# A two-layer encoder on one core: token block 0 ahead of block 1 at each norm, attentions begun inside their projections, modulation rows and spare products taken off TensorE

## The chip, the cores and the metric

The kernel runs on one core of a Trainium2 chip. The core has TensorE (PE, matmuls), VectorE (DVE), ScalarE (ACT), GpSimd (POOL) and SyncE (SP, which here issues the weight transfers), each with its own instruction stream; they wait for each other on semaphores. The metric is the device time of one execution in microseconds (us), the median of several runs.

## The reference, cut to what matters

256 tokens of width 1024 go through two layers. Every sub-layer is modulated by rows computed from a conditioning vector c.

```python
x = x + gate * diff_attention(modulate(rms_norm(x, g), shift, scale), ...)   # layer 0, mixer A, 8 heads, 2 maps each
x = x + gate * swiglu(modulate(...), w_in, w_out)                            # layer 0, dense, D_FF = 2816
k, v = split(modulate(rms_norm(x, g), shift, scale) @ w_kv)                  # one shared K/V set
x = x + gate * window_attention(modulate(...), w_q, sinks, w_o, k, v)        # layer 1, mixer B, 16 heads
x = x + gate * moe_swiglu(modulate(...))                                     # layer 1, top 2 of 8 experts
```

Each shift, scale and gate is a row `c @ ada_w[:, 1024 columns] + ada_b`. In mixer B a head's softmax is `exp(l - m) / (sum(exp(l - m)) + exp(sink - m))` with `m = max(max(l), sink)`. Attention is causal by chunks of 64 tokens, so queries of tokens 0 to 127 see no key behind token 127.

## The kernel before, in words

**Tiling.** The tokens are two blocks of 128 (`TB` = 2; X, H and Q are 128 x 2 x 1024). Weights come as fp32 tiles of 128 x 1024 in a ring of 12 slots (WRAW). ACT rounds each to fp32r (`hi`, tile WHI, L642), DVE takes the rest (`lo`, tile WLO, L970), and PE multiplies every tile three times (WHI by the high and low parts of the activations, WLO by the high part; all recorded at L1471). The activations are transposed on PE (L1501), split into HT_HI by ACT (L704) and into HT_LO by DVE (L1036, L1038, four operations of 512 columns).

**Stages, in the order in which every engine's stream is written:** start and first norm; QKV (24 tiles); attention A (16 steps, block 0's eight heads first); WO (8 tiles); the residual and the norm; FFN (11 steps of 4 input and 2 output tiles); residual and norm; KV (4 tiles); a second norm; BQ (8); attention B (16 steps); BO (8); norm; router; MoE (56 steps of 8 + 4 tiles). WO, BQ and BO are `project`: for each weight tile both token blocks, 12 products of 128 x 512, so that both blocks end with the last tile. Behind each projection DVE runs `residual` (L1119, L1120, two of each), `rms` with ACT's squares (L655) and root (L671), `norm` (L1025, L1027, two of each); PE transposes H when both blocks are there, and its next product waits for all four HT_LO.

**Modulation rows.** A row is the sum of 8 pieces (128 x 1024 of ada_w times c). Most pieces are one operation each on DVE: `early_product` (L984) up to WO, and `products` (L995) in FFN, where POOL brings them into SHR; `FF_PRODUCTS` says how many go into each FFN step. A row so made is summed over partitions by PE (`mod_sums`, MOD times ones) and copied by ACT (`mod_rows`, L698). Three rows are made on PE itself, as WRAW times c in two halves a piece: row scale_f of layer 0 in attention A and gate_f of layer 1 in attention B (`row_pieces`, nine products a half, one or two per attention step), and scale_f of layer 1 behind FFN (`ada_on_pe`, 18 products).

**Spare products.** `keep_clock` issues products that nobody reads, 24, 40, 24 and 44 of them: ahead of WO, behind WO, behind BQ and behind BO.

```python
            mod_sums(3, MOD0[3], 2)
            keep_clock(0, 40)
            pe.wait_ge(mod_ready, MOD_READY_EARLY)
            ht_transposes(H, h_ready, (5, 6))
            pe.wait_ge(ht_lo, 12)
```

**Attention step n.** PE makes head n + 3's logits, the transposes of n's probabilities and the values' product of n - 1; DVE adds the bias to head n + 2's logits (L1068), takes the negated maximum (L1074 in A, L1077 and a minimum with the sinks, L1078, in B), then n's totals (L1088 to L1091 in A; L1094, L1095 in B), and in B scales the output of n - 2 (L1100); ACT takes the exponentials (L726; in B two of the sinks at L723 as well) and copies.

## Time and profile before

| what | value |
|---|---|
| median of 3 runs | 1586.43 us (1586.08 to 1592.24) |
| the profiled execution's own time | 1585.24 us |
| its span, first to last instruction | 1583.4 us |
| mean granted TensorE clock | 0.978 of full |
| TensorE busy | 1500.0 us |
| VectorE busy | 1282.0 us |
| ScalarE busy | 983.4 us |

The profiled execution took 1.84 us more than its span, and 1.19 us less than the median. Busy time doesn't count waits, so an engine's share says how full its stream is, not that it sets the end.

### The profile page before, as it was taken

What the parts mean: (1) busy time and instruction counts of PE and PEld (TensorE: products, weight loads), DVE (VectorE), ACT (ScalarE), POOL (GpSimd) and SP (SyncE); (2) the same over time, 40 slices, a digit from 0 to 9 for tenths busy, and PEclk for the clock granted to TensorE, in tenths of its full rate; (3) what the DMA queues carried; (4) which work ended last, traced back from release to release, by engine and by line L of the source; (5) the groups of instructions that cost most, each with busy time, mean ns of one, the idle gap of its engine ahead of it and who ended that gap; (6) DMA issues with size and microseconds to landing.
All of it is one profiled execution on the core that took longest, in us unless ns stands there. A gap on an engine that the chain in (4) does not pass through costs nothing.

```text
span 1583.4 us, 22553 instructions
## 1 busy us (share of the span) xinstructions
PE 1500.0 (95%) x6706; PEld 1192.2 (75%) x6706; DVE 1282.0 (81%) x1396; ACT 983.4 (62%) x1276; POOL 83.6 (5%) x119
## 2 busy tenths in 40 slices
PE   5898989999978996999999999999999999999997
PEld 2784768777656575888888888888888888888886
DVE  5776758788655655989989989989989989989997
ACT  2466423444335623678778778778778778778774
POOL 3000121111010000000000000000000000000100
PEclk9999989999989998999999999999999999999999
DMA  9972479898474332999999999999999999999994
GB/s 344 347 275 73 145 251 371 296 348 310 152 231 145 113 125 83 343 373 369 395 379 370 394 380 365 396 377 367 398 378 370 392 376 372 381 376 370 398 392 167
DMA packets 212226, 494.33 MB, mean 312 GB/s; under 512 B 16434, under 2 KB 39186, under 8 KB 212178
## 3 DMA queue, kind: packets, MB, share of 16 engines
q1 hardware_dynamic: 198000, 444.66, 77.0%
q0 software_dynamic: 13376, 47.03, 8.5%
q10 hardware_dynamic: 802, 2.06, 0.3%
q8 instruction: 25, 0.41, 0.1%
q14 instruction: 23, 0.18, 0.0%
HBM read 487.13 MB, written 6.55 MB: 312 GB/s over the span
## 4 chain that ended last, share of the span: by engine, by line
PE 88%; DVE 7%; DMA 2%; ACT 2%; issue 1%; SPq 0%; DVEq 0%; ACTq 0%
PE PS L1471 85%; DMA WRAW<-in_ada_w 2%; PE PS L1861 2%; DVE HT_LO L1036 1%; DVE WLO L970 1%; PE PS L1569 1%; DVE MOD L995 0%; ACT WHI L642 0%; DVE ss L1045 0%; PE PS L1839 0%; DVE H L1025 0%; DVE X L1120 0%; DVE H L1027 0%; DVE Q L1054 0%; PE PS L1700 0%
## 5 line engine op out<-in xcount | busy, mean ns | idle before, releaser
L970 DVE TENSOR_TENSOR WLO<-WRAW,WHI 128x1024 fp32r<-128x1024 f32 x790 | 915.5, 1218 | 92.6 <-ACT WHI L642 92.4
L642 ACT ACTIVATE WHI<-WRAW 128x1024 fp32r<-128x1024 f32 x790 | 778.4, 1052 | 100.1 <-PE PS L1471 64.0
L1471 PE MATMUL PS<-WHI,HT_HI 128*128 128x512 f32 x1280 | 513.6, 401 | 26.8 <-DVE WLO L970 12.7
L1471 PE MATMUL PS<-WLO,HT_HI 128*128 128x512 f32 x1280 | 504.4, 394 | 0.0
L1471 PE MATMUL PS<-WHI,HT_LO 128*128 128x512 f32 x1280 | 431.1, 394 | 0.0
L1471 PEld LDWEIGHTS PS<-WHI,HT_HI 128*128 128x128 f32 x1280 | 244.0, 191 | 79.2 <-DVE HT_LO L1036 12.2
L1471 PEld LDWEIGHTS PS<-WHI,HT_LO 128*128 128x128 f32 x1280 | 243.5, 190 | 52.9
L1471 PEld LDWEIGHTS PS<-WLO,HT_HI 128*128 128x128 f32 x1280 | 244.3, 191 | 48.5
L1471 PE MATMUL PS<-WHI,AT_HI 128*128 128x512 f32 x536 | 214.2, 400 | 4.4 <-DVE WLO L970 3.0
L1471 PE MATMUL PS<-WHI,AT_LO 128*128 128x512 f32 x536 | 209.5, 391 | 0.0
L1471 PE MATMUL PS<-WLO,AT_HI 128*128 128x512 f32 x536 | 209.5, 391 | 0.0
L921 ACT ACTIVATE AT_HI<-PS 128x512 fp32r<-128x512 f32 x56 | 33.5, 599 | 190.1 <-PE PS L1861 190.1
L1471 PEld LDWEIGHTS PS<-WHI,AT_HI 128*128 128x128 f32 x536 | 101.1, 189 | 28.5 <-issue 4.6
L1471 PEld LDWEIGHTS PS<-WLO,AT_HI 128*128 128x128 f32 x536 | 101.0, 188 | 23.7 <-issue 2.9
L1471 PEld LDWEIGHTS PS<-WHI,AT_LO 128*128 128x128 f32 x536 | 101.0, 188 | 21.1
L1395 DVE TENSOR_TENSOR AT_LO<-PS,AT_HI 128x512 fp32r<-128x512 f32 x56 | 38.7, 692 | 72.2 <-ACT AT_HI L921 72.2
L995 DVE SCALAR_TENSOR_TENSOR MOD<-SHR,condT,MOD 128x1024 f32<-128x1024 f32 x56 | 71.6, 1278 | 0.6
L1471 PE MATMUL PS<-WRAW,condT 128*128 128x512 f32 x108 | 56.5, 640 | 2.1 <-DMA WRAW<-in_ada_w 2.1
L836 ACT ACTIVATE AT_HI<-PS 128x512 fp32r<-128x512 f32 x11 | 6.6, 599 | 63.7 <-PE PS L1700 63.7
L610 POOL DMA_DIRECT2D y_rows<-MOD x7 | 4.0, 574 | 797.1 <-DVE MOD L1382 797.1
L1471 PE MATMUL PS<-MOD,CST 128*128 128x512 f32 x64 | 35.5, 666 | 9.0 <-DMA MOD<-in_ada_b 5.4
L1391 DVE TENSOR_TENSOR MOD<-MOD,PS 128x512 f32<-128x512 f32 x56 | 38.0, 679 | 6.4 <-ACT MOD L917 6.4
(209 smaller groups left out, 880.5 us busy)
## 6 DMA issues: line engine op xcount, KB each, us to landing
WRAW<-in_moe_w_in SPq DMA_DIRECT2D x448, 512.0 KB, 6.3
WRAW<-in_moe_w_out SPq DMA_DIRECT2D x224, 512.0 KB, 5.5
WRAW<-in_ada_w SPq DMA_DIRECT2D x56, 512.0 KB, 6.9
WRAW<-in_ffn_w_in SPq DMA_DIRECT2D x88, 256.0 KB, 5.8
SHR<-in_ada_w POOLq DMA_DIRECT2D x40, 512.0 KB, 6.4
WRAW<-in_a_w_qkv SPq DMA_DIRECT2D x24, 512.0 KB, 16.3
WRAW<-in_ffn_w_out SPq DMA_DIRECT2D x22, 512.0 KB, 5.9
SHR<-in_kv_ada_w POOLq DMA_DIRECT2D x16, 512.0 KB, 6.1
```

The lines of the kernel that those rows point to most:

```text
L610: pool.dma_start(Y_ROWS.ap()[e * P:(e + 1) * P, :], Y).then_inc(y_stored, 16)
L642: nc.scalar.activation(WHI[:, u.split(k), :], WRAW[:, u.raw(k), :], ACT.Copy).then_inc(w_hi, 1)
L836: nc.scalar.activation(AT_HI[:, :], PS[:, 2, :], ACT.Copy).then_inc(at_hi, 1)
L921: nc.scalar.activation(AT_HI[:, :], PS[:, 2, :], ACT.Copy).then_inc(e_at_hi, 1)
L970: V_.tensor_tensor(WLO[:, u.split(k), :], WRAW[:, u.raw(k), :], f32(WHI[:, u.split(k), :]), ALU.subtract).then_inc(w_lo, 1)
L995: V_.scalar_tensor_tensor(row, ADA[:, k % ADA_SLOTS, :], condT[:, k:k + 1], row, ALU.mult, ALU.add).then_inc(ada_used, 1)
L1036: V_.tensor_tensor(dst, PS[:, b, :], high, ALU.subtract).then_inc(ht_lo, 1)
L1391: V_.tensor_tensor(EACT, ESIL, PS[:, 1, :], ALU.mult).then_inc(e_act, 1)
L1395: V_.tensor_tensor(AT_LO[:, :], PS[:, 2, :], f32(AT_HI[:, :]), ALU.subtract).then_inc(e_at, 1)
L1471: return nc.tensor.matmul(out, a, b, start=start, stop=stop)
L1569: last = nc.tensor.transpose(PS[:, 4 + n % 2, at:at + P], s_buf(a, n)[:, m, kt * P:(kt + 1) * P], ident)
L1861: last = nc.tensor.transpose(PS[:, 2, c * P:(c + 1) * P], EACT[:, c * P:(c + 1) * P], ident)
```

## The change

1. The four `keep_clock` calls go (132 products).
2. Row scale_f of layer 1 goes to DVE's `products` in FFN (`FF_PRODUCTS` of the last four entries 7 for 5), and POOL loads its pieces. Of row scale_f of layer 0, pieces 0 to 3 go to DVE in QKV (`SCALE_AT`), 4 to 7 stay on PE (`scale_pieces`). Row gate_f goes to DVE behind attention B (`gate_products`).
3. WO, BQ and BO are `project_by_block`: tiles 0 and 1 for both blocks, tiles 2 to 7 for block 0, then the same for block 1. FFN's last two tiles are ordered so too. `residual`, `rms` and `norm` run per block, the norm in halves of 512 columns, each of which releases four transposes; a projection's first products wait for their own HT_LO alone.
4. Attention A's first four heads' logits are issued among V's last tiles. Inside BQ's block 1, block 0's queries are transposed and heads 0 and 1 get their logits; block 1's queries are transposed in attention step 1. In both attentions block 0's outputs are normed or transposed ahead of the last steps.
5. In B the sink is a 129th (257th) logits column: a zero in PSUM and the sink in the bias tile. The exponential's sum then holds it; four small operations a head go.
6. POOL issues the small loads of the start after ten DVE products, and the attention's bias load after six `lo`.

```diff
-FF_PRODUCTS = (6, 6, 6, 6, 6, 6, 5, 5, 5, 5)
+FF_PRODUCTS = (6, 6, 6, 6, 6, 6, 7, 7, 7, 7)
...
+SCALE_PE = tuple((SCALE_F0, k) for k in range(4, KT))
 GATE_AT = tuple(range(4, 20, 2))
+SCALE_AT = (17, 19, 21, 23)
...
-    order += list(range(U_FF, U_KV)) + [("scale_f", k) for k in range(KT)]
-    order += list(range(U_KV, U_BO + 5)) + [("gate_f", k) for k in range(KT)]
+    order += list(range(U_FF, U_BO + 5)) + [("gate_f", k) for k in range(KT)]
...
                     for m in range(2):
-                        if a == "B":
-                            nc.scalar.activation(c[:, 6 + m:7 + m],
-                                                 sinks[:, 2 * (n % HEADS) + m:2 * (n % HEADS) + m + 1], ACT.Exp,
-                                                 bias=c[:, 2 + m:3 + m], scale=-1.0)
-                        nc.scalar.activation(buf[:, m, 0:span], buf[:, m, 0:span], ACT.Exp,
+                        nc.scalar.activation(buf[:, m, 0:cols], buf[:, m, 0:cols], ACT.Exp,
                                              bias=c[:, 2 + m:3 + m],
                                              accum_out=c[:, 4 + m:5 + m]).then_inc(sems["expd"], 1)
 
...
+                    if n == 1 and a == "B":
+                        transposed(10, lambda n: Q[:, 1, n * 512:n * 512 + 512], 3, (6, 7), qkt_psum)
...
+            def gate_products(*ks):
+
+                row = MOD[:, LATE_SLOTS[LATE_GATE_F], :]
+                for k in ks:
+                    place = PLACE["gate_f", k]
+                    dve.wait_ge(w_landed[place % RAW_SLOTS], landed_at(place))
+                    dve.wait_ge(ada_used, DVE_FF + k)
+                    V_.scalar_tensor_tensor(row, WRAW[:, place % RAW_SLOTS, :], condT[:, k:k + 1], row,
+                                            ALU.mult, ALU.add).then_inc(ada_used, 1)
...
-            def norm(scale_slot, shift, gains):
+            def norm(i, scale_slot, shift, gains):
 
                 dve.wait_ge(gain_used, gains)
-                for i in range(TB):
-                    chain(V_.scalar_tensor_tensor(H[:, i, :], X[:, i, :], nx[:, i, 1:2], MOD[:, scale_slot, :],
-                                                  ALU.mult, ALU.mult))
-                    V_.tensor_tensor(H[:, i, :], H[:, i, :], shift, ALU.add
+                for half in range(2):
+                    cols = slice(half * 512, half * 512 + 512)
+                    chain(V_.scalar_tensor_tensor(H[:, i, cols], X[:, i, cols], nx[:, i, 1:2],
+                                                  MOD[:, scale_slot, cols], ALU.mult, ALU.mult))
+                    V_.tensor_tensor(H[:, i, cols], H[:, i, cols], shift[:, cols], ALU.add
                                      ).then_inc(h_ready, 1)
...
+            dve.wait_ge(block_out, 1)
+            dve.wait_ge(mod_ready, MOD_READY_EARLY - 2)
+            residual(0, MOD0[2])
+            fold(MOD0[4], MOD[:, MOD0[4], :], 2)
+            rms(0, 3)
+            dve.wait_ge(mod_ready, MOD_READY_EARLY)
...
-            dve.wait_ge(mod_ready, MOD_READY_EARLY - 2)
-            residual(lambda i: pair(4 + 2 * i), MOD0[2], lambda i: H[:, i, :])
-            fold(MOD0[4], MOD[:, MOD0[4], :], 2)
-            rms(4)
-            dve.wait_ge(mod_ready, MOD_READY_EARLY)
-            norm(MOD0[4], MOD[:, MOD0[3], :], 2)
+            residual(1, MOD0[2])
+            lo(u, 32)
+            rms(1, 4)
...
             lo(u, *range(0, 6))
+            dve.wait_ge(mod_ready, MOD_READY_EARLY + 2 * LATE_SHIFT_F)
+            fold(MODKV[1], MOD[:, MODKV[1], :], 3)
+            dve.wait_ge(block_out, 2)
+            residual(0, MOD0[5])
             dve.wait_ge(w_used, U_KV)
-            dve.wait_ge(mod_ready, MOD_READY_EARLY + 2 * LATE_SHIFT_F)
-            residual(lambda i: pair(4 + 2 * i), MOD0[5], lambda i: H[:, i, :])
...
-            norm(MOD1[1], MOD[:, MOD1[0], :], 4)
-            head_norm(7, 4, 64, lambda i: heads_of(PS[:, 4 + i, 0:256], 4),
-                      lambda i: [KDUP[:, i, :, c, :] for c in range(2)], kdup_ready)
+            for i in range(TB):
+                norm(i, MOD1[1], MOD[:, MOD1[0], :], 4)
+            u = Units(U_BQ)
+            lo(u, 0, 1)
             ht_los(4)
-            u = Units(U_BQ)
-            lo(u, *range(0, 13))
-            head_norm(9, 16, 64, lambda i: heads_of(pair(4 + 2 * i), 16),
...
+            biased("B", 0)
+            biased("B", 1)
+            head_norm(1, 9, 16, 64, W4[:, :], [(heads_of(Q[:, 1, :], 16), heads_of(pair(6), 16), 0, 16)], qk_norm)
             attention("B")
             ht_los(5)
-            lo(u, *range(13, 20))
+            lo(u, 12, 13)
+            gate_products(0, 1, 2)
+            lo(u, 14)
+            gate_products(3, 4)
+            lo(u, 15)
+            gate_products(5, 6, 7)
             dve.wait_ge(wr_hi_ready, 1)
...
+            def project_by_block(u, bank, splits, between):
+
+                project(u, 0, bank, range(0, 2), splits)
+                if (0, 1) in between:
+                    between[0, 1]()
                 for i in range(TB):
-                    pe.wait_ge(ready, counts[i])
-                    for k in range(KT):
+                    for k in range(2, KT):
+                        if i == 0:
+                            split_ready(u, k)
+                            pe.wait_ge(ht_lo, splits + k // 2 + 1)
+                        last = block_products(u, k, i, bank)
+                        if i:
+                            last.then_inc(w_used, 1)
+                            if (1, k) in between:
+                                between[1, k]()
+                    if i == 0:
+                        last.then_inc(block_out, 1)
...
-            def keep_clock(bank, count):
-
-                for _ in range(count):
-                    mm(PS[:, bank, :], HT_HI[:, 0, 0:P], HT_HI[:, 0:2, :].rearrange("p k s -> p (k s)"))
...
+            def scale_pieces(n):
+
+                for half, steps in enumerate(SCALE_STEPS):
+                    cols = slice(half * 512, half * 512 + 512)
+                    for at, k in steps:
...
-            attention("A")
-            mod_sums(2, MOD0[2], 4)
+            logits("A", 0, 1)
+            project(u, 2 * KT, 4, range(6, 7))
+            logits("A", 2)
+            project(u, 2 * KT, 4, range(7, 8))
+            logits("A", 3)
+            attention("A", 4)
+            mod_sums(DVE_QKV, MOD0[2], 4)
+            ht_transposes(Q, h_parts(1, BLOCKS[:2]))
             pe.wait_ge(attn["A"]["o_ready"], TB * HEADS)
-            keep_clock(0, 24)
-            ht_transposes(Q, h_ready, (3, 4))
-            pe.wait_ge(ht_lo, 8)
+            ht_transposes(Q, h_parts(1, BLOCKS[2:]))
             pe.wait_ge(mod_ready, MOD_READY_EARLY - 2)
-            project(Units(U_WO), 0, 4)
-            mod_sums(3, MOD0[3], 2)
-            keep_clock(0, 40)
+            project_by_block(Units(U_WO), 4, 4, {(1, 3): lambda: mod_sums(DVE_EARLY, MOD0[3], 2)})
             pe.wait_ge(mod_ready, MOD_READY_EARLY)
-            ht_transposes(H, h_ready, (5, 6))
-            pe.wait_ge(ht_lo, 12)
-
-            def f_in(u, k0, ks, first, last):
+            ht_transposes(H, h_parts(2, BLOCKS[:2]))
+            ht_transposes(H, h_parts(2, BLOCKS[2:]))
...
-            mod_sums(ADA_EARLY + LATE_SHIFT_F, MOD1[3], 2)
-            ada_on_pe(0, 0)
+            mod_sums(DVE_FF - KT, LATE_SLOTS[LATE_SHIFT_F], 0)
+            mod_sums(DVE_FF, LATE_SLOTS[LATE_SCALE_F], 2)
             pe.wait_ge(mod_ready, MOD_READY_EARLY + 2 * (LATE_SCALE_F + 1))
-
-
-            ht_transposes(H, h_ready, (7, 8))
-            pe.wait_ge(ht_lo, 16)
+            ht_transposes(H, h_parts(3, BLOCKS[:2]))
+            pe.wait_ge(x_new, 4)
+            ht_transposes(H, h_parts(3, BLOCKS[2:]))
...
-            keep_clock(3, 24)
...
-            keep_clock(3, 44)
...
+            def first_queries():
+
+                pe.wait_ge(qk_norm, 5)
+                block_transposes(Q, 0, 4, qkt_psum)
+
+            def first_logits():
+
+                pe.wait_ge(qkt_ready, 10)
+                pe.wait_ge(kbt_ready, 2)
+                pe.wait_ge(sink_cols, 1)
+                logits("B", 0, 1)
+
+            project_by_block(Units(U_BQ), 4, 16,
+                             {(0, 1): kbt_transposes, (1, 5): first_queries, (1, 6): first_logits})
+            logits("B", 2)
+            attention("B", 3)
+            ht_transposes(Q, [(1, half, attn["B"]["o_ready"], HEADS + 4 * half + 4) for half in range(2)])
+            project_by_block(Units(U_BO), 4, 20, {})
+            ht_transposes(H, h_parts(5, BLOCKS[:2]))
+            pe.wait_ge(x_new, 6)
+            mod_sums(DVE_FF + KT, LATE_SLOTS[LATE_GATE_F], 6)
+            ht_transposes(H, h_parts(5, BLOCKS[2:]))
```

**VectorE around WO's end.** H<-PS and X<-X,H are the residual, nx the root's scalars, H<-X,nx,MOD and H<-H,MOD the norm. Of before:

```order
L970 TENSOR_TENSOR WLO<-WRAW,WHI 128x1024 [waits w_hi] x4
L1119 TENSOR_TENSOR H<-PS,MOD 128x1024 [waits mod_ready,w_used]
L1120 TENSOR_TENSOR X<-X,H 128x1024 [waits dve_chain]
L1119 TENSOR_TENSOR H<-PS,MOD 128x1024
L1120 TENSOR_TENSOR X<-X,H 128x1024 [waits dve_chain]
L1018 SCALAR_TENSOR_TENSOR MOD<-MOD,S 128x1024 [waits gain_landed]
L1007 TENSOR_SCALAR nx<-nx 128x2 [waits x_squares]
L1010 RECIPROCAL nx<-nx 128x2 [waits root_ready]
L1025 SCALAR_TENSOR_TENSOR H<-X,nx,MOD 128x1024 [waits gain_used,mod_ready,dve_chain]
L1027 TENSOR_TENSOR H<-H,MOD 128x1024 [waits dve_chain]
L1025 SCALAR_TENSOR_TENSOR H<-X,nx,MOD 128x1024
L1027 TENSOR_TENSOR H<-H,MOD 128x1024 [waits dve_chain]
L1036 TENSOR_TENSOR HT_LO<-PS,HT_HI 128x512 [waits ht_hi] x4
```

Of the change, from the residual of block 1 on (block 0's residual, scalars and norm stand in the nine rows ahead):

```order
L1144 TENSOR_TENSOR H<-PS,MOD 128x1024 [waits w_used]
L1145 TENSOR_TENSOR X<-X,H 128x1024 [waits dve_chain]
L997 TENSOR_TENSOR WLO<-WRAW,WHI 128x1024 [waits w_hi]
L1044 TENSOR_SCALAR nx<-nx 128x1 [waits x_squares]
L1047 RECIPROCAL nx<-nx 128x1 [waits root_ready]
L1063 SCALAR_TENSOR_TENSOR H<-X,nx,MOD 128x512 [waits gain_used,dve_chain]
L1065 TENSOR_TENSOR H<-H,MOD 128x512 [waits dve_chain]
L1063 SCALAR_TENSOR_TENSOR H<-X,nx,MOD 128x512
L1065 TENSOR_TENSOR H<-H,MOD 128x512 [waits dve_chain]
L997 TENSOR_TENSOR WLO<-WRAW,WHI 128x1024 [waits w_hi]
L1074 TENSOR_TENSOR HT_LO<-PS,HT_HI 128x512 [waits ht_hi] x4
```

Half of the residual and of the norm has moved ahead of the wait for WO's last tile; three of four `lo` now follow it.

**TensorE behind FFN's last product.** MOD,CST are sums of rows over partitions, WRAW,condT pieces of a row, CST,H transposes. Of before (the first five of the eight pairs of pieces):

```order
L1471 MATMUL PS<-WHI,AT_LO 128x512
L1471 MATMUL PS<-MOD,CST 128x512 [waits ada_used,mod_ready]
L1471 MATMUL PS<-MOD,CST 128x512
L1471 MATMUL PS<-MOD,CST 128x512 [waits modb_landed]
L1471 MATMUL PS<-MOD,CST 128x512
L1471 MATMUL PS<-WRAW,condT 128x512 [waits w_landed6]
L1471 MATMUL PS<-WRAW,condT 128x512
L1471 MATMUL PS<-WRAW,condT 128x512 [waits w_landed7]
L1471 MATMUL PS<-WRAW,condT 128x512
L1471 MATMUL PS<-WRAW,condT 128x512 [waits w_landed8]
```

Of the change:

```order
L1540 MATMUL PS<-WHI,AT_LO 128x512
L1540 MATMUL PS<-MOD,CST 128x512 [waits ada_used,mod_ready]
L1540 MATMUL PS<-MOD,CST 128x512
L1540 MATMUL PS<-MOD,CST 128x512 [waits ada_used]
L1540 MATMUL PS<-MOD,CST 128x512
L1597 MATMUL PS<-CST,H 128x128 [waits h_ready,mod_ready]
L1597 MATMUL PS<-CST,H 128x128 x3
L1597 MATMUL PS<-CST,H 128x128 [waits h_ready]
L1597 MATMUL PS<-CST,H 128x128 x3
```

The two sums of row scale_f took the place of 18 products, and the transposes go in four parts.

**VectorE between attention B and the residual behind BO.** Of before:

```order
L1100 TENSOR_TENSOR Q<-PS,sm 128x128 [waits pv_B] x2
L1036 TENSOR_TENSOR HT_LO<-PS,HT_HI 128x512 [waits ht_hi] x4
L970 TENSOR_TENSOR WLO<-WRAW,WHI 128x1024 [waits w_hi] x7
L1271 TENSOR_TENSOR wr_lo<-wr,wr_hi 128x64 [waits wr_hi_ready]
L1119 TENSOR_TENSOR H<-PS,MOD 128x1024 [waits w_used]
L1120 TENSOR_TENSOR X<-X,H 128x1024 [waits dve_chain]
L1119 TENSOR_TENSOR H<-PS,MOD 128x1024
```

Of the change:

```order
L1128 TENSOR_TENSOR Q<-PS,sm 128x128 [waits pv_B] x2
L1074 TENSOR_TENSOR HT_LO<-PS,HT_HI 128x512 [waits ht_hi] x4
L997 TENSOR_TENSOR WLO<-WRAW,WHI 128x1024 [waits w_hi] x2
L1021 SCALAR_TENSOR_TENSOR MOD<-WRAW,condT,MOD 128x1024 [waits ada_used,w_landed11]
L1021 SCALAR_TENSOR_TENSOR MOD<-WRAW,condT,MOD 128x1024 [waits ada_used,w_landed0]
L1021 SCALAR_TENSOR_TENSOR MOD<-WRAW,condT,MOD 128x1024 [waits ada_used,w_landed1]
L997 TENSOR_TENSOR WLO<-WRAW,WHI 128x1024 [waits w_hi]
L1021 SCALAR_TENSOR_TENSOR MOD<-WRAW,condT,MOD 128x1024 [waits ada_used,w_landed2]
L1021 SCALAR_TENSOR_TENSOR MOD<-WRAW,condT,MOD 128x1024 [waits ada_used,w_landed3]
L997 TENSOR_TENSOR WLO<-WRAW,WHI 128x1024 [waits w_hi]
L1021 SCALAR_TENSOR_TENSOR MOD<-WRAW,condT,MOD 128x1024 [waits ada_used,w_landed4]
L1021 SCALAR_TENSOR_TENSOR MOD<-WRAW,condT,MOD 128x1024 [waits ada_used,w_landed5]
```

Eight products of gate_f stand among the `lo` of BO's tiles 4 to 7.

## Rows read from the trace of the kernel before

**Rows 1.** The page's fourth part: the chain that ended last, share by engine.

```profile
PE 88%; DVE 7%; DMA 2%; ACT 2%; issue 1%; SPq 0%; DVEq 0%; ACTq 0%
```

**Rows 2.** Windows cut at TensorE's starts: length, busy by engine, PEclk, DMA share, GB/s.

```profile
46.53:121.38 74.85, 72.70 (x338) 59.99 (x339) 55.14 (x67) 39.28 (x56) 0.95 (x1) 0.98 0.86 308
125.33:172.38 47.05, 40.90 (x191) 23.45 (x190) 32.16 (x79) 31.66 (x94) 4.55 (x4) 0.96 0.32 101
172.38:212.76 40.38, 36.53 (x156) 29.05 (x157) 32.94 (x31) 13.86 (x18) 3.82 (x4) 0.96 0.64 206
212.76:418.51 205.75, 196.56 (x836) 155.75 (x837) 152.28 (x140) 79.25 (x99) 30.42 (x58) 0.98 0.84 299
418.51:448.66 30.15, 26.43 (x81) 14.86 (x81) 19.43 (x21) 11.54 (x17) 3.14 (x5) 0.94 0.66 178
461.53:493.81 32.28, 26.95 (x121) 22.52 (x120) 20.72 (x27) 18.04 (x26) 0.00 (x0) 0.89 0.58 204
493.81:554.67 60.86, 53.05 (x301) 34.40 (x299) 36.60 (x109) 40.45 (x131) 0.57 (x1) 0.97 0.28 85
554.67:595.07 40.40, 35.84 (x157) 29.09 (x157) 22.33 (x24) 12.18 (x18) 1.09 (x2) 0.96 0.38 121
641.44:1583.40 941.96, 934.03 (x4239) 771.27 (x4237) 847.09 (x792) 706.28 (x776) 17.90 (x16) 1.00 1.00 371
```

**Rows 3.** The chain of work, WO's products to FFN's first: start, length, what.

```profile
172.38 23.69 PE PS L1471 x96
...
196.09 1.24 DVE H L1119
...
204.06 1.30 DVE H L1025
...
210.22 2.49 DVE HT_LO L1036 x4
```

**Rows 4.** PE's timeline before FFN; in brackets the idle time before, and its releaser.

```profile
197.20 9.68 PE L1471 MATMUL PS<-HT_HI 128*128 128x512 f32 x40
...
212.76 0.50 PE L1471 MATMUL PS<-WHI,HT_HI 128*128 128x512 f32 x1 [2.55 <-DVE HT_LO L1036]
```

**Rows 5.** Windows of 2 us for PE: length, busy, PEclk (granted clock), DMA share, GB/s.

```profile
212.00:214.00 2.00, 1.24 (x5) 1.00 0.34 116
214.00:216.00 2.00, 2.00 (x6) 0.51 0.67 214
```

**Rows 6.** DVE's timeline in attention A, block 1: `biased` of two heads in a row.

```profile
141.92 0.68 DVE L1068 TENSOR_TENSOR S<-PS,SHR 128x512 f32<-128x512 f32 x1
...
147.02 0.69 DVE L1068 TENSOR_TENSOR S<-PS,SHR 128x512 f32<-128x512 f32 x1 [2.85 <-PE PS L1471]
```

**Rows 7.** DVE's timeline in a step of the dense channel mixer.

```profile
300.02 2.67 DVE L995 SCALAR_TENSOR_TENSOR MOD<-SHR,condT,MOD 128x1024 f32<-128x1024 f32 x2
```

**Rows 8.** DVE's timeline at that mixer's end: the split of the last tiles.

```profile
417.14 4.63 DVE L970 TENSOR_TENSOR WLO<-WRAW,WHI 128x1024 fp32r<-128x1024 f32 x4 [0.25 <-ACT WHI L642]
```

**Rows 9.** PE's timeline behind that mixer's last product.

```profile
429.07 13.90 PE L1471 MATMUL PS<-WRAW,condT 128*128 128x512 f32 x32
```

**Rows 10.** The chain from BQ's last product to attention B's first transpose.

```profile
493.81 1.04 ACT W L796
...
507.47 0.64 PE PS L1569 x2
```

**Rows 11.** PE's timeline in attention B, block 1.

```profile
532.16 1.02 PE L1471 MATMUL PS<-WRAW,condT 128*128 128x512 f32 x2
...
533.11 0.70 PE L1471 MATMUL PS<-MOD,Q 64*128 64x256 f32 x4
...
536.08 0.70 PE L1471 MATMUL PS<-MOD,Q 64*128 64x256 f32 x4
```

**Rows 12.** DVE's timeline in attention B, block 1: `biased` of two heads in a row.

```profile
527.99 0.68 DVE L1068 TENSOR_TENSOR MOD<-PS,SHR 128x512 f32<-128x512 f32 x1
...
530.10 0.68 DVE L1068 TENSOR_TENSOR S<-PS,SHR 128x512 f32<-128x512 f32 x1
```

More of the change, by code:

```diff
@@ L1480, in split_ready, with block_products @@
                 pe.wait_ge(w_lo, u.count(k) + 1)
-            def project(u, k0, bank, ks=range(KT)):
+            def block_products(u, k, i, bank):
+                s, rows = u.split(k), slice(i * P, i * P + P)
+                kt = k % KT
+                for half in range(2):
+                    cols = slice(half * 512, half * 512 + 512)
+                    last = split_mm(PS[:, bank + 2 * i + half, :], HT_HI[:, kt, rows], HT_LO[:, kt, rows],
+                                    WHI[:, s, cols], WLO[:, s, cols], kt == 0, kt == KT - 1)
+                return last
@@ L1685, in f_in @@
+            def f_in(u, k0, ks, first, last, splits=None):
                 for k in ks:
```

542 lines of the change are left out of this document (297 added, 245 removed).

## The prediction

> **What bounds the kernel now.** I read the page's chain first: TensorE holds 88% of what ended last, VectorE 7% [rows 1]. Then the stages, cut where TensorE starts [rows 2]. MoE, 942 of 1583 us, keeps PE busy for 934 at full clock with the DMA engines at 1.00; the change alters nothing in it, so it stays. What can move lies ahead of 595 us, and there the stages differ. In FFN PE is busy for 197 of 206 us and DVE for 152: PE is the bound, DVE's slack is small. Between the projections the engines take turns: from WO's first product to FFN's takes 40.38 us, of which WO's products are 23.69, and behind them stand the residual, the norm and four HT_LO [rows 3]. Attention B takes 60.86 us with PE busy for 53, attention A 47.05.
>
> A product costs 0.2275 us at full clock: MoE's window holds 4032 of them and 224 transposes of a quarter of the columns, for which I take half that time each. WO's 96 would be 21.8 us and took 23.69, so a start at half clock costs 1.9 us. The spare products do not prevent it: 40 ran from 197.20 for 9.68 us, the transposes followed, PE paused 2.55 us for HT_LO [rows 4], the granted clock was still 1.00 in the window at 212 and fell to 0.51 in the next, after products had begun again [rows 5]. The Trainium skill ("TensorE: Matmul & The Clock Gate", section "Why this matters for your kernels") advises to keep TensorE fed without pauses between bursts, which speaks against removing the spare products; by these rows they bought nothing at the one place that they were for.
>
> **The change part by part.** All against the profiled execution's 1585.24 us (span 1583.4 and 1.84 around it; 1.2 below the median of the runs).
>
> (a) *Start and QKV: 0.* QKV waits for its first HT_LO instead of four and for half norms: PE may start 4 to 5 us earlier. But DVE takes four more products of 1.28 us (half of 2.67 [rows 7]), 5 us, in a window in which it is busy 55 of 75 us, and the norms of Q and K, for which V's tiles and the logits wait, stand behind them. The later bias load relieves the weights. I let gain and loss cancel; the ends are -5 (all of the start kept) and +3.
>
> (b) *Attention A to WO: -9.* The window is 47.05 [rows 2]. The row's last eight half products remain of sixteen, and are spread: 8 x 0.87 (a half product is two records, 13.90/16 [rows 9]) = 7 us less on PE. Where PE was idle it fell to half clock: DVE waited 2.85 us for one head's logits and the step took 5.10 instead of some 2.2 [rows 6]; I count that once as saved, 2.9, and 2.5 for steps that PE paced. Behind the last step, squares and scalars of block 0 are now done early, the norm releases four transposes at a time and WO waits for one HT_LO (three of four saved, 2.49 for four [rows 3], 1.9): 3.6 in all. Ends -4 (DVE and ACT, busy 32 each, pace all steps) and -11.
>
> (c) *WO to FFN: -6.2.* Block 0's residual (2.46) and norm (2.5) go under block 1's 36 products (8.2 us). PE's 96 products and the sum take 23.7 + 1.7; then come residual of block 1 2.46 [rows 3], a `lo` 1.2, scalars 0.7, norm 2.6, a `lo` 1.2, HT_HI and one HT_LO 0.6 each: 9.4 less 0.6 of overlap with the sum. Together 34.2 against 40.38. The two `lo` that now stand in the chain are price of the new order. Ends -3 (block 0's norm late, behind the sum) and -8. The 40 spare products cost nothing before, since PE waited for the norm anyway; so their going gives nothing here.
>
> (d) *FFN: +6.* Eight more products at 1.28 on DVE: 10.2 us if DVE paced every step. In steps with a sum and 6 products DVE has hardly a pause from tile to tile, two products in a row among them [rows 7]; over the whole stage it is idle for 53 of 206 us [rows 2]. The last four steps get two each. Two of them have a sum and I count +1.9 each; one has none, +0.5; in the last the sum is near and I take +1.7. Ends +4 and +10.2. DMA brings 4 MB more in these steps, on top of 299 GB/s.
>
> (e) *Behind FFN to KV: -10.5.* The window of 30.15 loses 16 half products, 13.90 us [rows 9], and two more that add the bias row, 1.7; two more sums (1.7) come. DVE becomes the chain: `lo` of the six tiles at 1.16 each from 417.14 on [rows 8] end 5.6 us into the window, then fold 1.2, two residuals 4.9, scalars 0.5, two norms 5.1, HT_HI, HT_LO and the last transposes 1.7, some 0.5 between: 19.6. So of the 15.5 taken off PE only 10.5 is seen. Ends -12 (PE paces) and -8.
>
> (f) *KV to BQ's end: 0.* KV's copy frees PSUM and BQ starts some 6 us sooner, but PE then waits for KDUP, whose norm now stands behind two more `lo`, restarts at half clock, and takes on the transposes of block 0's queries and two logits. Ends -3 and +3.
>
> (g) *Attention B: -21*, the largest term. Before, 13.66 us pass between BQ's last product and the first transpose of probabilities [rows 10]: two head norms, the query transposes, `biased`, exponentials. Of that block 0's half now runs in BQ; the window's start to step 2 I count as 10.8, since block 1's head norm, the Exp table and its transposes still come. Block 1's steps were paced by PE at 2.97 us (533.11 to 536.08), of which 0.87 is a piece; without it PE needs 2.1 [rows 11]. DVE's step was 2.11 (527.99 to 530.10) with the two sink operations [rows 12]; without them I take 2.0. Block 0's steps I take at 1.5. So 10.8 + 4 x 1.5 + 8 x 2.0 + the last two 2.6, last product to BO 2.6, half-clock restart 1.9: 39.9 against 60.86. In what is left, 18 half products (15.6 us) are the main thing. Ends -16 and -25.
>
> (h) *BO to router: -5.5.* As (c), but eight gate products of 1.28 stand on DVE between `lo` of BO's tiles. DVE is busy 22.3 of 40.4, so it has the room, yet block 0's residual comes late: its 60 products end at 15.5 (13.6 and a cold start), but DVE has three HT_LO 1.9, four `lo` 4.7, eight products 10.2 and the fold 1.2 ahead of it, 18.3 with the small split of the router's weights. Residual, scalars, squares, norm and a `lo` bring it to 26.3, behind PE's last product at 23.7; the tail as in (c), 8.6, ends at 34.9 against 40.40. 44 spare products cost nothing, PE waited. Ends -2 (the products push the tiles' `lo`, and BO waits) and -8.
>
> (i) Router and MoE: 0. The zero column in PSUM and the copy of the sinks are two small DVE operations in BQ, where DVE is busy for 20.7 of 32.3 us; without that cover they would cost under 1 us.
>
> Sum: 0 - 9 - 6.2 + 6 - 10.5 + 0 - 21 - 5.5 = -46.2, which gives **1539.0 us**. All cheap ends at once would give 1517, all dear ones 1568; since they hardly go together I take 1524 to 1560 for the likeliest case.
>
> **The rivals.**
>
> *Hand-offs move to VectorE and give most back* (0.10). DVE gets 20 products more (25.6 us) and the `lo` stand in the chains of (c), (e), (h). If FFN takes the full +10.2, attention A's steps stay at DVE's pace (-4), (c) and (h) give -3 and -2, (e) -8, (g) -16 and (a) +2: -20.8, 1564 us. For it: DVE is busy 152 of 206 in FFN. Against: it has pauses where the chains lie.
>
> *Slower: TensorE stays at half clock* (0.03). Without spare products the pauses at four hand-offs might leave whole projections slow. A product at half clock costs 0.2 us more; WO, BQ and BO wholly so cost 3 x (96 x 0.2 - 1.9) = 52, so 1591 us. It decides from about 230 products at half clock that are not so now. For it: pauses of 2.5 us precede every fall. Against: the falls happened with the spare products too, and each is over within some 4 us of products, 1.9 us of loss a time [rows 3, 5]. The skill's advice (same page and section) is this rival; the trace does not bear it out.
>
> *More than forecast* (0.05): block 0's chains are wholly hidden and V does not wait for K's norm: all cheap ends but FFN's, -5 - 11 - 8 + 6 - 12 - 3 - 25 - 8 = -66, 1519 us, with 1524 as the near edge. For it: DVE's share between projections is a half. Against: each `lo` in a tail is a wait that was not there.
>
> *The change does little* (0.02): only if the sixteen half products and the pieces had been in shadow already; rows 9 and 11 speak against it, since PE has no gap there.
>
> **How the numbers follow.** The likeliest case has 0.80, at 1539, own range 1524 to 1560. The dear case lies just above, the cheap one just below, so 1524 to 1560 leaves out some 2 in 10 and is my range. A measurement of this kernel tells a change from none at about 0.5%, 8 us. Every case but the second and the last is faster by more: 0.95, and I leave 0.02 for the same and 0.03 for slower.
>
> **What would show each step.** Time from WO's first product to FFN's of 34, from FFN's end to KV's start of 20, from BQ's last product to BO's first of 40; AT transposes in FFN's last four steps 1 to 2 us further apart. In attention B, block 1's logits every 2.0 us. Granted clock back at full within 4 us of every start. The forecast is wrong if DVE's idle time vanishes in QKV or if BQ's block 1 waits for KDUP longer than some 4 us, if gate products hold `lo` of BO's tiles, or if clock rows show 0.5 for a whole projection.

## The result and the profile after

The changed kernel took 1569.17 us (median of 4 runs, 1564.66 to 1575.25) beside 1586.26 for the kernel before: 0.9905 of its time, 95% interval 0.9878 to 0.9931. In a later session of 12 runs it took 1577.84 (1558.46 to 1583.17), 0.9936 [0.9904, 0.9967]. A ratio, here and below, is estimated from the fast runs beside those of the kernel before in the same session and is not the quotient of two medians; one of the 12, 1583.17, counts as slow. The change is faster by 1% or less, 17 us in the first session and some 10 by the ratio of the second, where 46 were forecast, and both times are outside the range of 1524 to 1560. In the later session its single runs scatter over 25 us, those of the kernel before over 12.

The profiled execution took 1564.66 us, span 1562.8. In the chain of work on its profile page VectorE's share has grown from 7% [rows 1] to 12%.

```profile
PE 81%; DVE 12%; issue 2%; DMA 2%; ACT 2%; SPq 0%; DVEq 0%; ACTq 0%
```

The windows, with columns as in [rows 2]. In order: QKV's first product to WO; WO to FFN; FFN; its last tiles to KV; KV to the end of BQ's products; attention B, up to BO's first product; BO to the router; router to MoE's steady part; MoE.

```profile
41.53:162.65 121.12, 107.04 (x496) 77.40 (x497) 94.49 (x155) 71.67 (x154) 5.68 (x7) 0.97 0.68 235
162.65:197.56 34.91, 27.88 (x117) 20.91 (x117) 32.32 (x37) 15.01 (x22) 5.33 (x4) 0.91 0.63 195
197.56:411.14 213.58, 199.50 (x836) 155.07 (x837) 165.40 (x152) 79.74 (x99) 35.54 (x68) 0.98 0.88 315
411.14:431.28 20.14, 15.02 (x48) 10.86 (x49) 18.28 (x24) 10.70 (x18) 3.16 (x5) 0.78 0.94 266
431.28:472.49 41.21, 38.55 (x184) 30.68 (x185) 31.03 (x46) 20.02 (x30) 3.67 (x3) 1.00 0.46 139
472.49:509.73 37.24, 30.89 (x226) 24.24 (x225) 26.24 (x69) 28.86 (x92) 0.57 (x1) 0.95 0.12 42
509.73:545.07 35.34, 29.41 (x117) 21.07 (x118) 32.59 (x38) 13.02 (x21) 1.09 (x2) 0.90 0.70 229
545.07:597.08 52.01, 38.74 (x181) 32.81 (x182) 29.55 (x77) 17.02 (x21) 1.98 (x2) 0.77 0.38 128
597.08:1562.80 965.72, 958.02 (x4243) 771.56 (x4241) 847.23 (x792) 707.23 (x776) 17.79 (x16) 1.00 0.98 362
```

Of the kernel before, the windows that [rows 2] does not have in this cut: KV to the end of BQ's products, attention B, router to MoE's steady part.

```profile
448.66:493.61 44.95, 39.62 (x169) 32.76 (x170) 26.73 (x32) 18.04 (x25) 3.65 (x3) 0.89 0.71 243
493.61:554.67 61.06, 53.25 (x302) 34.59 (x300) 36.60 (x109) 40.45 (x131) 0.57 (x1) 0.97 0.28 85
595.07:641.44 46.37, 35.09 (x185) 29.49 (x186) 26.80 (x73) 14.82 (x18) 1.98 (x2) 0.82 0.34 114
```

| stage | before | after | moved | forecast |
|---|---|---|---|---|
| start to WO (a, b) | 172.38 | 162.65 | -9.7 | -9 |
| WO to FFN (c) | 40.38 | 34.91 | -5.5 | -6.2 |
| FFN (d) | 205.75 | 213.58 | +7.8 | +6 |
| FFN's last tiles to KV (e) | 30.15 | 20.14 | -10.0 | -10.5 |
| KV to BQ's last product (f) | 44.95 | 41.21 | -3.7 | 0 |
| attention B (g) | 61.06 | 37.24 | -23.8 | -21 |
| BO to router (h) | 40.40 | 35.34 | -5.1 | -5.5 |
| router to MoE's steady part | 46.37 | 52.01 | +5.6 | 0 |
| MoE | 941.96 | 965.72 | +23.8 | 0 |

At the router the kernel is 50 us ahead. Then MoE, which the change does not touch, takes 23.8 us more, with the same work (x4243 records beside x4239) at a granted clock of 1.00, as before. In the stretch below TensorE is busy throughout in both kernels and simply makes fewer products. It is the same stretch of MoE in the kernel before and in the changed one, for PE alone (busy, records, clock, DMA share, GB/s). Before:

```profile
700.00:1000.00 300.00, 300.00 (x1371) 1.00 1.02 379
```

After:

```profile
700.00:1000.00 300.00, 300.00 (x1338) 1.00 1.01 374
```

2.4% fewer products in 300 us. The 4032 products of MoE take 23.8/4032 = 0.0059 us more each. The rate is already lower in QKV: from 60 to 110 us the products of HT start 0.233 us apart (mean of those that follow each other without a break), before 0.227.

### The profile page after: what moved, and what is told of

It is laid out like the page before. It is cut to its first block, busy times and chain, and to the rows that moved or that the text cites. A ratio compares the mean times of both kernels' runs of the same rounds, so it can differ in the third digit from the quotient of the medians.

```text
span 1562.8 us, 22184 instructions
## 1 busy us (share of the span) xinstructions
PE 1470.3 (94%) x6494; PEld 1155.3 (74%) x6494; DVE 1303.6 (83%) x1411; ACT 976.6 (62%) x1246; POOL 87.2 (6%) x127
## 4 chain that ended last, share of the span: by engine, by line
PE 81%; DVE 12%; issue 2%; DMA 2%; ACT 2%; SPq 0%; DVEq 0%; ACTq 0%
PE PS L1540 77%; DVE WLO L997 2%; PE PS L1983 2%; DVE MOD L1011 1%; DVE MOD L1032 1%; DMA WRAW<-in_a_w_qkv 1%; DMA WRAW<-in_ada_w 1%; DVE HT_LO L1074 1%; ACT WHI L657 1%; DVE MOD L1021 1%; PE PS L1666 1%; DVE ss L1082 0%; DVE X L1145 0%; DVE H L1063 0%; PE PS L1609 0%
## 5 line engine op out<-in xcount | busy, mean ns | idle before, releaser
L1540 PE MATMUL PS<-WLO,HT_HI 128*128 128x512 f32 x1280 | 510.1, 399 | 0.0
L1540 PE MATMUL PS<-WHI,HT_LO 128*128 128x512 f32 x1280 | 436.1, 397 | 0.0
L1540 PE MATMUL PS<-WHI,AT_HI 128*128 128x512 f32 x536 | 217.7, 406 | 4.4 <-DVE WLO L997 3.0
L1032 DVE SCALAR_TENSOR_TENSOR MOD<-SHR,condT,MOD 128x1024 f32<-128x1024 f32 x64 | 81.9, 1280 | 1.8 <-DVE MOD L1032 0.5
L1540 PE MATMUL PS<-MOD,CST 128*128 128x512 f32 x64 | 38.1, 713 | 10.5 <-DMA MOD<-in_ada_b 4.6
L944 ACT ACTIVATE MOD<-PS 128x512 f32<-128x512 f32 x56 | 33.5, 599 | 22.1 <-PE PS L1540 22.1
L1011 DVE SCALAR_TENSOR_TENSOR MOD<-WRAW,condT,MOD 128x1024 f32<-128x1024 f32 x31 | 39.7, 1282 | 6.2 <-DMA WRAW<-in_ada_w 5.3
```

Source lines behind the costliest of these rows:

```text
L944: nc.scalar.activation(ESIL, PS[:, 0, :], ACT.Silu).then_inc(e_silu, 1)
L1011: V_.scalar_tensor_tensor(row, piece, condT[:, k:k + 1], row, ALU.mult, ALU.add).then_inc(ada_used, 1)
L1032: V_.scalar_tensor_tensor(row, ADA[:, k % ADA_SLOTS, :], condT[:, k:k + 1], row, ALU.mult, ALU.add).then_inc(ada_used, 1)
L1540: return nc.tensor.matmul(out, a, b, start=start, stop=stop)
```

## The experiments

**Where the slower products come from.** The tile SHR was widened by 16 columns for the sinks (`SHR = sb("SHR", [P, 4 * D + NBIAS])`), and every tile allocated behind it, X, H, HT_HI, HT_LO, AT_HI and AT_LO among them, moved by 64 bytes a partition. A product has a stationary operand, here HT or AT, and a moving one, WHI or WLO. Four kernels were run together: the shift alone in the kernel before, the changed kernel realigned, the changed kernel again, and one with spare products (told below).

```diff
-        SHR = sb("SHR", [P, 4 * D])
+        SHR = sb("SHR", [P, 4 * D + NBIAS])
```

> The kernel before with one thing changed: the tile SHR is 16 columns (64 bytes a partition) wider, and nothing uses them. X, H, the HT and AT tiles and everything allocated behind SHR move by 64 bytes. Theory A (the addresses are why the changed kernel's TensorE starts a product every 0.233 us instead of every 0.2275): MoE's products come 0.233 apart here too, 4032 of them cost 22 us, and with the other stages the run takes 1.5 to 2% longer than before, about 1612 us. Theory B (it has nothing to do with addresses, but with the chip, the single execution or with what runs beside): 0.2275 apart and 1586 us, within 0.3%.

Measured: 1618.09 us (6 runs), 1.0216 [1.0191, 1.0242], and 1334 records in the 300 us: the loss is there without the rest of the change. About 5450 products (4032 in MoE, 792 in FFN, 624 in the projections) at 0.006 us are 33 us, and 34 were lost.

```diff
-        SHR = sb("SHR", [P, 4 * D + NBIAS])
+        SHR = sb("SHR", [P, 4 * D + 256])
```

> The changed kernel with SHR 240 columns wider than it has it (256 beyond the 4096), nothing uses them, so the tiles behind SHR begin on a multiple of 1024 bytes again. Theory A: products 0.2275 apart in MoE, some 24 us back there and 5 to 8 ahead of it, about 1540 us, which is what I had forecast for the change. Theory B: no difference from the changed kernel, 1565 to 1575 us, 0.233 apart.

Measured: 1551.04 us (6 runs, 1538.74 to 1556.34), 0.978 [0.9744, 0.9816]. Its profiled execution has a span of 1538.0; the windows of FFN, of attention B, of the router and of MoE are:

```profile
198.66:409.00 210.34, 195.90 (x836) 155.11 (x837) 165.29 (x152) 79.75 (x99) 35.68 (x68) 0.98 0.90 320
...
469.66:513.54 43.88, 37.88 (x225) 29.84 (x225) 26.71 (x69) 29.36 (x92) 0.57 (x1) 0.73 0.11 39
...
548.88:596.48 47.60, 34.38 (x186) 29.55 (x187) 29.54 (x77) 17.11 (x22) 1.98 (x2) 0.82 0.43 138
596.48:1538.02 941.54, 933.89 (x4238) 771.09 (x4236) 847.17 (x792) 706.56 (x776) 18.07 (x16) 1.00 1.00 371
```

MoE is back at 941.5 us. Theory A holds in both directions. But the median is 12 us above the forecast, attention B took 43.88 here and 37.24 in the changed kernel, and six runs spread over 18 us: something else is in play.

> The changed kernel once more, unaltered. If the slower spacing of products belongs to the kernel (theory A, or anything else that the change does), it is there again, 0.233 us in MoE, and the time is 1565 to 1575 us. If it belonged to the chip or the execution (theory B), the spacing is 0.2275 and the time near 1540.

Measured: 1577.84 us (12 runs), 0.9936 [0.9904, 0.9967], 1336 records in the 300 us. The low rate belongs to the kernel, theory B is out. Its profiled execution has a span of 1572.7, ten more than the first, and the difference is attention B. Its window, cut as above:

```profile
471.51:522.76 51.25, 45.39 (x226) 36.01 (x225) 26.72 (x69) 29.01 (x92) 0.57 (x1) 0.60 0.09 33
```

The single runs follow the clock. Of the 12, the three with a mean granted clock of 0.976 to 0.980 took 1558.46 to 1565.30 us, the nine with 0.963 to 0.968 took 1574.47 to 1583.17; the four of the first session part in the same way (0.977: 1564.66 and 1566.86; 0.969 and 0.967: 1571.48 and 1575.25). The first profiled execution is one of the quick kind, this one of the others.

**Which tiles, and what grain.** Two runs shift only some tiles of the kernel before.

```diff
+        PAD0 = sb("PAD0", [P, 16])
         AT_HI = sb("AT_HI", [P, 512], F32R)
```

> The kernel before with an unused tile of 16 columns (64 bytes) ahead of AT_HI: AT_HI, AT_LO and what is allocated behind them move by 64 bytes, while SHR, X, H, HT_HI and HT_LO stay. If a product is slower when its stationary operand is off by 64 bytes, only the products of AT are 0.233 us apart and those of HT stay at 0.2275: 1344 products in MoE and 264 in FFN at 0.006 more, some 9 to 10 us, 1593 us. If something else behind SHR is the cause (CST, a gain tile), all products are slow or none.

Measured: 1594.12 us (7 runs), 1.0057 [1.0032, 1.0081], as expected for AT's 1608 products alone. Its trace says so by tile: from 700 to 1000 us AT's products start 0.2335 us apart (before 0.2266), HT's 0.2281 as before. So it is the tile that the product reads as its stationary operand that counts, not something else behind SHR.

```diff
+        PAD0 = sb("PAD0", [P, 16])
         WHI = sb("WHI", [P, SPLIT_SLOTS, UNIT], F32R)
         WLO = sb("WLO", [P, SPLIT_SLOTS, UNIT], F32R)
+        PAD1 = sb("PAD1", [P, 240])
```

> The kernel before with 16 unused columns ahead of WHI and 240 behind WLO: the moving operands WHI and WLO are off by 64 bytes, all tiles behind them keep the alignment of before. If only the stationary operand matters, 0.2275 us a product and 1584 us. If any operand of the product off by 64 bytes slows it, 0.233 and 1610 us or more.

Measured: 1595.92 us (4 runs), 1.0068 [1.004, 1.0097]. Neither expectation: the moving operand matters too, but a third as much, 12.5 us over 5450 products, 0.002 us each, where the stationary one costs 0.006. By tile, HT's products are 0.001 us further apart than before and AT's 0.002. I had given it nothing or all.

Four more widths of SHR in the kernel before, the same edit with another number:

> The kernel before with SHR 8 columns (32 bytes) wider. If the loss comes with any shift that is no multiple of 128 bytes, it is there as with 64, 1618 us and 0.233 us a product. If 32 bytes are the grain, nothing changes, 1584 us, but then 64 bytes should not have mattered either, so I expect the loss.

> The kernel before with SHR 32 columns (128 bytes) wider: X, H, HT, AT and what follows off by 128 bytes. If a multiple of 128 bytes is enough for a product at 0.2275 us, nothing changes, 1584 us. If the 1024 or 256 bytes are needed that the realigned kernel has, some or all of the 2% of the 64-byte shift are there, 1595 to 1618 us.

> The kernel before with SHR 64 columns (256 bytes) wider. 128 bytes cost 1.9%, 1024 bytes nothing. If the grain is 256 bytes, 1584 us and 0.2275 us a product; if it is 512 or 1024, 1.5 to 2% more, about 1613.

> The kernel before with SHR 128 columns (512 bytes) wider. If the grain is 256 or 512 bytes, 1584 us; if it is 1024, about 1613.

| SHR wider by | runs | median us | ratio to before | records in 300 us of MoE |
|---|---|---|---|---|
| 0 | 9 to 29 a session | 1582.6 to 1583.9 | 1 | 1371 |
| 32 bytes | 2 | 1617.78 | 1.0211 [1.0184, 1.0239] | 1335 |
| 64 bytes | 6 | 1618.09 | 1.0216 [1.0191, 1.0242] | 1334 |
| 128 bytes | 2 | 1613.94 | 1.0187 [1.0162, 1.0212] | 1338 |
| 256 bytes | 8 | 1586.69 | 1.0018 [0.9993, 1.0043] | 1370 |
| 512 bytes | 8 | 1583.34 | 0.9997 [0.9979, 1.0016] | 1370 |

Of the shifts tried, those that are no multiple of 256 bytes cost 2%, and the others nothing.

**The spare products.** Those behind WO and behind BO were put back into the changed kernel.

```diff
             project_by_block(Units(U_WO), 4, 4, {(1, 3): lambda: mod_sums(DVE_EARLY, MOD0[3], 2)})
+            keep_clock(0, 40)
...
             project_by_block(Units(U_BO), 4, 20, {})
+            keep_clock(3, 44)
```

> The changed kernel with 84 of the 132 spare products back, 40 behind WO and 44 behind BO, where PE waits for the residual and the norm. My forecast's reading: they fall in PE's waiting time except for what overhangs it, so 0 to +4 us against the changed kernel, and the granted clock still falls to 0.5 within some us of FFN's first products. Rival (the spare products keep the clock up): FFN's and the router's first products run at full clock and the run is 2 to 6 us faster than the changed kernel.

Measured: 1578.44 us (12 runs), 0.9954 [0.9927, 0.9981], against 0.9936 for the changed kernel beside it: no difference that the intervals show. But my expectation on the clock was wrong. FFN began in the changed kernel at 197.56, at half clock:

```profile
198.00:200.00 2.00, 2.00 (x6) 0.50 0.80 264
200.00:202.00 2.00, 2.00 (x8) 0.63 0.69 227
```

With the 40 spare products, whose last transposes are followed by only 1.45 us of waiting, it began at 202.00 and kept full clock:

```profile
202.00:204.00 2.00, 2.00 (x9) 1.00 0.61 196
204.00:206.00 2.00, 2.00 (x10) 1.00 0.82 274
```

So in this execution FFN did not start cold (at half clock). The router's first products ran at full clock too, but from there to MoE's steady part the clock was 0.77 and the time 52.1 us, as without them. And they overhang the waits: WO to FFN took 37.3 us with them and 34.9 without, BO to router 38.0 and 35.3, while FFN to the end of BQ's products took 274.8 and 274.9. By the stages they cost some 5 us. The single runs say the same once they are sorted by clock: the six with 0.978 to 0.982 took 1567.19 to 1574.84 (without spare products 1558.46 to 1565.30), the six with 0.969 to 0.972 took 1582.04 to 1587.32 (1574.47 to 1583.17). The medians are alike because the quick kind is 6 of 12 here and 3 of 12 there, and 12 runs each cannot tell that from chance.

**The clock in attention B.** Its granted clock was 0.95 in one execution of the changed kernel and 0.60 in the next. With the two levels, full (2.4 GHz) and half (1.2 GHz), that is half clock for 2 x (1 - clock) x window, 3.7 us and 41 us. The window is longer by 14.0 us, 0.38 for each us at half clock. Theory C: with the row's pieces gone, attention B's own small products do not bring the clock back, and the pause before the first transpose lets it fall. The pause, in the changed kernel:

```profile
477.67 0.45 PE L1666 MATMUL PS<-CST,MOD 128*128 128x128 f32 x2 [4.02 <-ACT MOD L730]
```

First, that pause of the realigned kernel filled:

```diff
                         logits(a, n + 3)
+                    if n == 0 and a == "B":
+                        keep_clock(5, 16)
                     transposes(n)
```

> The changed kernel with the tiles realigned (as in the run with SHR 256 columns wider) and 16 spare products issued into a free bank where TensorE waits some 4 us for the first exponentials of attention B. Theory C (that pause lets the granted clock fall, and attention B's small products without the row's pieces get it back only after 15 to 45 us): the clock is 1.00 in attention B from the start, the window from BQ's last product to BO's first is 5 to 12 us shorter, the median is about 1540 and the scatter of single runs shrinks from 18 us to a few. Rival (the half clock comes from somewhere else, or the spare products only delay the first transposes): 1551 us or more, scatter as before.

Measured: 1545.24 us (6 runs, 1534.31 to 1550.31), 0.9747 [0.9713, 0.9781]; not told from the realigned 0.978. In its trace that pause is closed; the longest one left in attention B is 1.89 us, and behind that one the clock fell all the same:

```profile
467.15 3.91 PE L1540 MATMUL PS<-HT_HI 128*128 128x512 f32 x16
...
475.20 0.66 PE L1540 MATMUL PS<-MOD,W 128*128 128x64 f32 x4 [1.89 <-ACT Q L718]
```

```profile
474.00:476.00 2.00, 0.80 (x6) 1.00 0.00 0
476.00:478.00 2.00, 2.00 (x16) 0.76 0.00 0
478.00:480.00 2.00, 2.00 (x11) 0.50 0.00 0
480.00:482.00 2.00, 2.00 (x10) 0.50 0.00 0
```

It stayed there while TensorE was busy without a break:

```profile
480.00:490.00 10.00, 10.00 (x41) 0.50 0.01 2
490.00:500.00 10.00, 10.00 (x44) 0.50 0.00 0
```

The half of theory C that puts it on that pause is not borne out. Whether the shorter one of 1.89 us is enough to let the clock fall was not tested. Then spare products in the steps, in bank 7 behind `products(n - 1)`: three in steps 2 to 7, two in steps 2 to 15, or one fp32 product in steps 2 to 15:

```diff
                         products(n - 1)
+                    if a == "B" and n >= 2:
+                        mm(PS[:, 7, :], ones, X[:, 0, 0:512])
```

> The same realigned kernel with three spare products in each of the steps 2 to 7 of attention B (18 in all), none in the pause. Theory C: the clock falls in the pause but comes back within the first steps as it did before when a piece stood in each step, 3 to 8 us faster than the realigned kernel in the median, about 1545, less scatter. Rival: 18 products cost 4 to 8 us on the path, 1555 us or more.

> The same with two spare fp32r products (0.23 us each at full clock) in each of the steps 2 to 15 instead, 28 products, 6.4 us. Theory C in its stronger form (a little dense work a step is enough): half clock for under 10 us, window 36 to 40 us, median 1540 to 1545. If it needs as much as the pieces were: half clock for 20 us and more, window 42 to 48 us, 1548 to 1555.

> The changed kernel, realigned, with one spare fp32 product of 512 columns in each of the steps 2 to 15 of attention B: as long as the piece of the modulation row that stood there before (0.87 us), 14 of them, 12 us. Theory C (attention B's own small products do not bring TensorE's granted clock back, what stood between them did): the half-clock stretch in attention B is some 4 to 7 us instead of 20 to 48, and the window from its first transpose to BO's first product is 42 to 45 us, much like the 39 to 49 that the half clock costs; the scatter of single runs is small. Rival (the long stretch is chance and the products don't matter): half-clock stretches of 20 us and more here too, and 50 us and more for the window.

> The changed kernel, realigned, with both sets of spare products in attention B: 16 in the pause before the first transpose and three in each of the steps 2 to 7. If the pause and the small products after it are both needed to keep the clock down, half clock for under 7 us, window 36 to 38 us, 1536 to 1541. If neither counts for much: half clock 20 to 30 us as in both single versions, 1545 to 1550.

| realigned kernel with | attention B, us | clock | at half, us | median us | ratio |
|---|---|---|---|---|---|
| nothing | 43.88 | 0.73 | 24 | 1551.04 | 0.978 [0.9744, 0.9816] |
| 16 in the pause | 49.36 | 0.69 | 31 | 1545.24 | 0.9747 [0.9713, 0.9781] |
| 3 in steps 2 to 7 | 47.09 | 0.78 | 21 | 1542.9 | 0.9753 [0.9723, 0.9784] |
| both of these | 43.37 | 0.92 | 7 | 1543.23 | 0.9744 [0.9718, 0.9771] |
| 2 in steps 2 to 15 | 53.47 | 0.71 | 31 | 1550.59 | 0.978 [0.9756, 0.9804] |
| 1 fp32 in steps 2 to 15 | 51.13 | 0.87 | 13 | 1553.06 | 0.9809 [0.979, 0.9828] |

The windows and clocks are of one execution each, the medians of 5 or 6 runs. None of the intervals parts from that of the realigned kernel. One fp32 product a step, the nearest to what stood there, had the stretch down to 13 us, not to the 4 to 7 that I expected, and runs within 7 us of each other; it costs as much as it saves. Three small ones in steps 2 to 7 left it at 21 us, where I expected the clock back within the first steps, and two small ones to the end at 31. With both sets it was 7 us, but the window was 43.37, not the 36 to 38 that I expected of that. The window of that kernel:

```profile
470.74:514.11 43.37, 40.09 (x259) 30.53 (x259) 26.64 (x69) 29.15 (x92) 0.57 (x1) 0.92 0.12 40
```

Last, the one part alone: the kernel before with its 18 half products of row gate_f in attention B (16 of pieces, two of the bias row) cut to one column. The row is not computed beyond these columns, so the result is wrong and the router may choose other experts.

```diff
-                    mm(PS[:, 7, :], ones, MOD[:, slot, half * 512:half * 512 + 512], True, False)
+                    thin = 1 if a == "B" else 512
+                    mm(PS[:, 7, 0:thin], ones, MOD[:, slot, half * 512:half * 512 + thin], True, False)
...
-                    last = mm(PS[:, 7, :], condT[:, k:k + 1].broadcast_to([P, P]),
-                              WRAW[:, place % RAW_SLOTS, half * 512:half * 512 + 512], False, k == KT - 1)
+                    thin = 1 if a == "B" else 512
+                    last = mm(PS[:, 7, 0:thin], condT[:, k:k + 1].broadcast_to([P, P]),
+                              WRAW[:, place % RAW_SLOTS, half * 512:half * 512 + thin], False, k == KT - 1)
```

> The kernel before with the pieces of row gate_f in attention B cut to one column of 512 each: the row's other columns are not computed, every instruction, wait and transfer stays. Theory C (without dense products attention B's own small ones leave the clock at half for long): the half-clock stretch in attention B grows from 3.4 us to 15 us or more, single runs scatter by 10 us and more, and of the 12 to 13 us that the pieces cost a part is lost: median 1574 to 1582. Rival (the long stretch comes from what the change does around attention B): 3.4 us stays, the window from the first transpose to BO's first product falls from 47.2 to about 35 us, median 1571 to 1573.

Measured: 1583.56 us (12 runs), 1.0009 [0.9986, 1.0031]. Its attention B, from BQ's last product on:

```profile
490.66:547.85 57.19, 49.68 (x302) 41.22 (x300) 36.79 (x109) 40.15 (x131) 0.57 (x1) 0.79 0.28 83
```

57.2 us beside 61.1 before, 24 us of them at half clock beside 3.7. At 0.38 the 20 us more cost 7.7 by estimate, so the thinner products were worth 3.9 + 7.7 = 11.6 in this window, and two thirds of that go to the clock. It is not one odd execution: 11 of the 12 runs have a mean granted clock of 0.968 to 0.970 and the twelfth 0.959, those of the kernel before beside them 0.973 to 0.982, 25 of 29 at 0.978 or more. So thinning the pieces alone lowers the clock, without anything else of the change. The rest of that gain was gone by MoE: its router window took 52.0 us at clock 0.72 (before 46.4 at 0.82), which may be the clock or the other routing. Of the expectations the scatter did not come: all but one run lie within 4 us.

## Why the prediction was wrong

**(i) MoE: 0. This is the step that failed.** The prediction said "the change alters nothing in it, so it stays": it alters no instruction there, but the addresses of their operands, by the 16 columns on SHR. That cost 23.8 us in MoE, and by estimate some 8 in the stages ahead (about 1420 products at 0.006). The realigned kernel, with MoE at 941.5, comes to 1551, inside the forecast range. The 12 us that still part it from 1539 I put down to the clock: two of its six runs took 1538.74 and 1539.84 at a mean clock of 0.974 and 0.973, the other four 1550.70 to 1556.34 at 0.961 to 0.966. That the quick ones hit the forecast is in part luck: in the traced one, whose span is 45.4 us shorter than before for 46.2 forecast, attention B gave 17.2 of 21 and (f) 4.4 for nothing. I had read the line as a place for the sinks and looked at no tile's address. None of my rivals had it.

**(g) Attention B, the step that was mis-priced.** In the profiled execution the mechanism held and was a little better than forecast: -23.8 for -21, 37.2 us for 39.9; block 1's logits came 1.7 to 2.1 us apart, for 2.0. But I priced a cold start at 1.9 us from starts of projections [rows 3, 5], where 512-column products follow at once. Even there "over within some 4 us" was too narrow: BQ's window of before, 32.28 us at 0.89 [rows 2], has 7 us at half clock. In attention B the stretch at half clock was 3.7 us in that execution and 24, 41 and 48 in those of the realigned kernel, of the repeat and of the one with 84 spare products; up to 17 us are lost. The rival that TensorE stays at half clock named this risk at the wrong place and for the wrong removal: it spoke of the spare products and of WO, BQ and BO, which recovered as forecast (clock 0.91 and 0.90 in (c) and (h), 1.00 in BQ). What lowered it was the removal of the pieces, which I had booked as a pure gain of 15.6 us. The Trainium skill ("TensorE: Matmul & The Clock Gate", section "Why this matters for your kernels") advises to avoid idle gaps of TensorE between bursts of products; that alone did not help here, since with the 4 us pause filled and none over 1.89 us left the clock fell too.

**(a), (b): right as a sum,** -9.7 for -9; their split was not as told: the start kept its 5.0 (QKV's first product at 41.53 for 46.53), and from there to WO the kernel gained 4.7. **(c), (e), (h)** came within 0.7, 0.5 and 0.4 us: residual and norm of block 0 do go under block 1's products, and behind FFN DVE is busy for 18.28 of 20.14 us, as the chain there should be. **(d)** was +7.8 for +6, of which the slower products are 3.2; realigned it is +4.6, near the cheap end. The last steps wait for DVE as forecast, here two of them:

```profile
348.64 0.47 PE L1540 MATMUL PS<-WHI,HT_HI 128*128 128x512 f32 x1 [2.24 <-DVE WLO L997]
...
370.06 0.47 PE L1540 MATMUL PS<-WHI,HT_HI 128*128 128x512 f32 x1 [2.24 <-DVE WLO L997]
```

**(f)** was 0 and is -3.7: PE waits 1.80 us for KDUP where I had some 4, and the clock did not fall.

```profile
452.96 1.06 PE L1891 MATMUL PS<-CST,MOD 128*128 128x128 f32 x8 [1.80 <-DVE MOD L1090]
```

**That spare products bought nothing** was right for the time and wrong for the reason. Back in the changed kernel, 40 of them kept the clock up at FFN's start in the traced execution, so it does not fall anyway; but the waits of the new order are too short for them, and 84 cost some 5 us where 0 to 4 were expected.

**Router to MoE: 0** was +5.6 in the changed kernel, at clock 0.77, and +1.2 in the realigned one, at 0.82 as before. That it is the clock is argued, not shown.

What stays open: why TensorE stays at half clock for 4 us in one execution and 48 in the next, in nearly the same instructions; whether both sets of spare products shorten it (the traced execution has the lowest mean clock of the six, 0.971 to 0.978, so it was not a lucky one, but other stages' cold stretches are in that mean too, and the median is not told from the realigned kernel's); and by what path an operand's address slows a product.

## What to carry to other kernels

Check where a change leaves the tiles behind the one that it resizes: here 64 bytes on one buffer, columns that TensorE never reads, cost 2% of the whole kernel, and padding it to a multiple of 1024 bytes gave that back (0.978 of the time before instead of 0.994); in the kernel before, a shift by 256 bytes cost nothing. When every product of a stage that the change doesn't touch is slower by the same share at full granted clock, look at addresses before looking at schedules. And work taken off TensorE in a stretch of small products is worth less than its duration: cut to one column, 15.6 us of half products gave no measurable time.
